# A second queue for the experts' down matrices: ACT asks for them, SP for the gate and up parts

## The reference

```python
def run(args):
    xi, e = args
    a, b = jnp.split(xi @ w_gu[e], 2, axis=-1)
    return (jax.nn.silu(a) * b) @ w_down[e]
```

## Time and profile before

| what | value |
|---|---|
| median of three runs | 842.99 us |
| the profiled execution, whole | 844.27 us |
| its span (first to last instruction) | 842.5 us |
| PE busy | 720.6 us (86%) |
| ACT busy | 152.2 us (18%) |
| q1 (SP's queue) | 230.96 MB |
| q10 (ACT's queue) | 6.54 MB |
| mean granted clock of PE | 0.982 of full speed |

### The profile page before, as it was taken

How to read it: one execution, slowest core, us unless ns; L and a number is a source line. 1 busy time by engine, 2 the same in 40 slices (tenths; PEclk the granted TensorE clock), 3 DMA queues, 4 the chain that set the end, 5 groups by cost and what they waited for, 6 DMA issues and landing times.

```text
span 842.5 us, 10234 instructions
## 1 busy us (share of the span) xinstructions
PE 720.6 (86%) x3647; PEld 373.2 (44%) x3647; DVE 203.0 (24%) x575; ACT 152.2 (18%) x363; POOL 182.4 (22%) x188
## 2 busy tenths in 40 slices
PE   6999999999988999499999997877777877877883
PEld 6788788778666446333333322222222222222220
DVE  2421305628495114710110101001001001001020
ACT  5223423033635211110000000000000000000000
POOL 5010000333000000123243241322232232232221
PEclk9999999999989999699999999999999999999998
DMA  9652942021700993499999999999999999999992
GB/s 302 123 152 69 280 159 59 1 77 34 268 1 5 391 420 140 160 348 414 408 408 417 402 406 412 418 408 414 413 408 412 416 409 412 415 414 410 415 413 73
DMA packets 76885, 246.52 MB, mean 293 GB/s; under 512 B 24944, under 2 KB 44303, under 8 KB 52235
## 3 DMA queue, kind: packets, MB, share of 16 engines
q1 hardware_dynamic: 63697, 230.96, 69.3%
q0 software_dynamic: 11776, 8.58, 4.6%
q10 hardware_dynamic: 1378, 6.54, 1.9%
HBM read 239.95 MB, written 24.92 MB: 314 GB/s over the span
## 4 chain that ended last, share of the span: by engine, by line
PE 42%; SPq 37%; DMA 9%; DVE 5%; issue 3%; ACT 2%; POOL 1%; ACTq 0%; POOLq 0%; DVEq 0%
PE bank L1111 40%; SPq L588 25%; SPq L595 11%; DMA reg_a<-in_exp_w_gu 3%; DMA reg_b<-in_exp_w_gu 3%; PE bank L1114 2%; DMA ffn_in<-reg_x 1%; DMA reg_x<-in_x_prompt 1%; DVE reg_a L1897 1%; DVE reg_y L2107 1%; DVE reg_b L1672 1%; DVE small L1857 1%; ACT reg_y L1094 0%; DVE reg_y L1904 0%; POOL small L693 0%
## 5 line engine op out<-in xcount | busy, mean ns | idle before, releaser
L1111 PE MATMUL bank<-reg_w,reg_y 128*64 128x512 f32 (+2 forms) x512 | 136.8, 572 | 15.7 <-DMA reg_w<-in_exp_w_gu 15.7
L1111 PE MATMUL bank<-reg_a,reg_y 128*64 128x512 f32 x528 | 122.8, 600 | 22.7 <-DMA reg_a<-in_exp_w_gu 17.0
L1111 PE MATMUL bank<-reg_b,reg_y 128*64 128x512 f32 x528 | 122.9, 600 | 21.4 <-DMA reg_b<-in_exp_w_gu 15.8
L2111 DVE TENSOR_TENSOR reg_y<-reg_y,bank 128x256 f32<-128x256 f32 x32 | 13.5, 421 | 417.1 <-ACT reg_y L1094 417.1
L1111 PEld LDWEIGHTS bank<-reg_w,reg_y 128*64 128x64 f32 (+2 forms) x512 | 45.3, 144 | 95.2 <-issue 54.1
L1111 PE MATMUL bank<-reg_b,reg_w 128*128 128x260 f32 x384 | 85.6, 383 | 0.0
L1111 PEld LDWEIGHTS bank<-reg_a,reg_y 128*64 128x64 f32 x528 | 34.3, 137 | 102.5 <-issue 49.4
L1111 PEld LDWEIGHTS bank<-reg_b,reg_y 128*64 128x64 f32 x528 | 34.6, 136 | 100.7 <-issue 57.8
L1111 PEld LDWEIGHTS bank<-reg_b,reg_w 128*128 128x128 f32 x384 | 72.6, 190 | 11.9 <-issue 1.0
L1114 PE MATMUL bank<-small,reg_y 128*128 128x128 f32 (+3 forms) x206 | 42.7, 317 | 24.6 <-DVE reg_y L2111 15.0
L1094 ACT ACTIVATE reg_y<-bank,small 128x256 f32<-128x256 f32 x32 | 15.2, 474 | 262.0 <-PE bank L1111 262.0
(11 more groups left out here) (357 smaller groups left out, 641.0 us busy)
## 6 DMA issues: line engine op xcount, KB each, us to landing
reg_a<-in_exp_w_gu SPq DMA_DIRECT2D x44, 1024.0 KB, 27.8
reg_b<-in_exp_w_gu SPq DMA_DIRECT2D x44, 1024.0 KB, 27.7
reg_w<-in_exp_w_gu SPq DMA_DIRECT2D x40, 1024.0 KB, 27.8
reg_a<-in_exp_w_down SPq DMA_DIRECT2D x22, 1024.0 KB, 28.1
reg_b<-in_exp_w_down SPq DMA_DIRECT2D x22, 1024.0 KB, 28.0
reg_h<-in_exp_w_down SPq DMA_DIRECT2D x20, 1024.0 KB, 27.8
reg_w<-in_w_in SPq DMA_DIRECT2D x9, 1024.0 KB, 10.7
reg_w<-in_w_out SPq DMA_DIRECT2D x2, 2048.0 KB, 11.0
```

Of the source, the lines that this page charges most:

```text
L1111: return eng.matmul(out, lhsT, rhs, start=start, stop=stop, skip_group_check=True)
L2111: tt(hid[b], silu[b], bank[2 + b][:, 256:512], ALU.mult).then_inc(S["hid_made"], 1)
```

## The change

SP no longer asks for the down matrices inside the loop. ACT gets a `load_down` of its own and asks for the two halves of expert e+3 after its silu of expert e, each behind the same wait as before, and then copies expert e's result. The loop of ACT is unrolled by six (three sets, two accumulators), with two experts ahead of it and six behind. The last three experts ask for nothing. The first three experts' matrices are still asked for by SP.

```diff
                     for g in range(3):
                         e = 3 * i + g
                         load_gu(e, g, first + e - 2)
-                        load_down(e, g, first + e - 2)
                 for e in range(N_EXP - N_EXP % 3, N_EXP):
                     load_gu(e, e % 3, first + e - 2)
-                    load_down(e, e % 3, first + e - 2)
...
-            def expert(e, n, b, reused=None):
+            def load_down(e, g, done):
+                for half in range(2):
+                    eng.wait_ge(down_half_done[half], done)
+                    src = down_dram[bass.ds(e, 1)].rearrange("e p s c n -> (e p) s c n")[:, half]
+                    eng.dma_start(down_w[g][:, half], src).then_inc(down_loaded[g][half], 16)
+
+            def expert(e, n, b, g, reused=None, more=True):
 
                 eng.wait_ge(S["gu_done"], n + 1)
                 eng.activation(silu[b], bank[2 + b][:, 0:256], ACT.Silu, scale=slot_scale[:, 1, bass.ds(e, 1)]).then_inc(S["silu_done"], 1)
+                if more:
+                    load_down(e + 3, g, n + 1)
                 eng.wait_ge(S["down_done"], n + 1)
...
-                for b in range(2):
-                    expert(b, N_EXP * r + b, b)
-                with eng.Fori(1, N_EXP // 2) as i:
-                    for b in range(2):
-                        expert(2 * i + b, N_EXP * r + 2 * i + b, b, 16 * N_EXP * r + 32 * i)
+                for e in range(2):
+                    expert(e, N_EXP * r + e, e, e)
+                with eng.Fori(0, 4) as i:
+                    for j in range(6):
+                        e = 6 * i + j + 2
+                        expert(e, N_EXP * r + e, j % 2, (j + 2) % 3, 16 * N_EXP * r + 96 * i + 32 * (j // 2) + 32)
+                for e in range(26, N_EXP):
+                    expert(e, N_EXP * r + e, e % 2, e % 3, 16 * N_EXP * r + 32 * (e // 2), e + 3 < N_EXP)
```

## The result

The changed kernel takes 851.52 us (median of four runs, 850.8 to 854.82); the kernel before took 843.65 us on the same chip. The ratio is 1.009, with an interval of 1.0066 to 1.0114: 7.9 us slower, where 7.5 were forecast. The profiled execution of the changed kernel is the longest of its four, 854.82 us with a span of 853.1. So its trace shows 10.55 us more than that of before (844.27), and its sizes are read with that in mind.

A forecast was written before the change was run, and what follows sets the result against it. The loop was taken as bound by DMA transfers without a gap. SP and ACT add 0 us and the later end 7.5 us: 842.99 + 7.5 = 850.5 us, range 840 to 862 us.

The forecast's parts named there:

- SP and ACT: Moving 58 load requests from SP to ACT in the loop was to cost or gain 0 us on either engine.
- The free price: Cost of one load request on ACT when its queue isn't held: 0.5 us, against 2.8 us when held.
- The order of the bytes: In the loop, down matrices on a second queue get half the rate, arriving in 14 us instead of 28, delaying gate and up parts.
- my sign of 12 to 16 us: Sign that the forecast is right: down halves in the loop land in 12 to 16 us instead of 28.
- The end: Gate and up parts of experts 30 and 31 come last; the last down product ends 5.5 to 8.2 us later.
- Rival A: Loop transfers: two queues feed the DMA engines better, at most 12.7 us gained, 838 us; chance 0.12.
- B: Loop loads: down halves come in the old order, so no change, 843 us; chance 0.10.
- D: Loop transfers: mixed traffic is carried worse, 381 for 412 GB/s, 24 us lost, 875 us; chance 0.08.
- C: In the loop POOL's adds become the bound, as a third queue lengthens turns: 10 us, 860 us; chance 0.12.
- the sign that I had named for C: In the loop, POOL starting its adds after a wait for the earlier ones; no size given.
- the 3 us to spare: In the loop, the time from the earlier adds' landing to POOL's start of the next expert's adds: 3 us.

## Why the prediction was right, point by point

*SP and ACT: 0 us.* Right. The kernel with 54 of 58 requests on ACT equals before. In ACT's timeline the copy follows the second request and is ready long before the next silu, as the earlier trace rows let one expect:

```profile
780.41 2.05 ACTq L1093 DMA_DIRECT2D reg_a<-in_exp_w_down  x2
782.56 0.69 ACT L1104 ACTIVATE reg_h<-bank,small 128x512 f32<-128x512 f32 x1 [5.67 <-PE bank L1120]
789.24 0.47 ACT L1098 ACTIVATE reg_y<-bank,small 128x256 f32<-128x256 f32 x1 [5.99 <-PE bank L1120]
```

The 2.05 us hold both requests, each of 0.34 us, and the wait for the down product between them. That product ended at 782.07 us, so the copy starts 0.49 us behind it, and 5.99 us stay idle before the silu. The free price was the right one to take, and a little high at 0.5 us: ACT's queue isn't held.

*The order of the bytes.* Right, in size too. I reckoned 14 us for a down matrix, 3.4 to start and 10.6 at half the rate. In the changed kernel ACT asks for one at 605.42 us; q10 moves nothing until some time in 608 to 609 us, and its last packets go in 619 to 620: some 3.4 and 10.6 us. The 11 us of the page are the median of single halves, each counted from its own request, so my sign of 12 to 16 us was set a little too high for them. Gate and up parts take 38 us. The queues of the changed kernel from 596 to 600 us (packets, MB, share):

```profile
q10 hardware_dynamic: 93, 0.76, 45.1%
q1 hardware_dynamic: 97, 0.70, 42.5%
q0 software_dynamic: 96, 0.11, 15.7%
```

Three queues take turns packet by packet, 93 to 97 to 96: each gets one turn in three, whether its packet is large or one of POOL's small ones. That each DMA engine goes round its queues packet by packet is the rule in the Trainium skill, "DMA: Bandwidth & Descriptors", section "Queues, rings and completion order", and the trace agrees.

*The end.* Right as a mechanism. One queue with the same fault at its end loses 5.8 and 9.4 us, two queues with the end in order lose nothing. Term by term, in the first profile: expert 29 complete at 806.36 us against 802.8 to 805.5; its way to the end of its down product 8.93 against 7.73 us, with the clock at 0.50; two more experts 25.77 against 25.34 us; sum 841.06 against 835.9 to 838.6. In the profile where the clock stays up on this stretch and the time is nearer to the median (852.29 us) the last down product ends at 838.53, at the upper edge of the forecast and some 11 us after the transfers, where 9 to 12 were forecast; in the other two profiles of the changed kernel it is 13 to 14 us. What follows it takes 853.1 - 841.06 = 12.0 us, before 842.5 - 830.41 = 12.1: unchanged, as said.

That the sum came out so near is partly luck, for two of its terms missed in opposite ways. I had the last down matrix asked for 8.2 us ahead of expert 29's last part, and 1.1 MiB of it missing then. In the first profile ACT asks for it from 793.22 us on, 13 us ahead, as that part comes late itself, and q10 moves only some 0.2 MB after 806 us. And I took up to one MiB off because most of the 16 engines would be ahead by then; but from 806.36 us to the transfers' end at about 828 lie 21.6 us, some 2.6 us for each of the 8.2 MiB that were left, so there was hardly anything to take off. One term too large by about a MiB and one taken off that wasn't there gave the lower edge of my 21.5 to 24.2 us, which is what came.

*Rival A* falls: 412 GB/s from 560 to 620 us, as before, and the transfers end no earlier. *B* falls: down halves land in 11 us. *D* falls: 412 GB/s with both queues at work. *C* came nearer than I gave it credit for. POOL's waits in the changed kernel (total us, times, longest):

```profile
POOL out_y_p L761 <- DMA out_y_s<-reg_y,reg_h: 97.4, 10, 10.9
...
POOL out_y_p L761 <- DMA out_y_s<-reg_h: 58.1, 6, 11.4
```

In 16 waits it was the earlier adds that POOL waited for, the sign that I had named for C; before, there was one such wait, of 8.0 us. So the turns did use up the 3 us to spare. But this sets no part of the loss: with the last two down matrices back in SP's list there are 18 such waits and no loss, and with half as many adds there is one such wait and a loss of 8.0 us.

*What stays open.* The kernel with two down matrices early lost 9.4 us where 6 us, up to some 7.6, had been expected. Its last down product ends at 840.37 us instead of 836.8. Of these 3.6 us some 1 is the later end of the transfers, and 0.6 the last expert, which takes 13.29 us from the end of the down product before (827.08 us) instead of 12.67. Its expert 30 was complete at 819.34 us; by the 2.66 us per MiB 4 MiB before its transfers' end at 828 us it would be 817.4. Why its last part let PE on 2 us later than that I didn't settle. Nor is it settled why the kernel with one down matrix early loses 5.8 us in the median and not 4.3.

## What to carry to other kernels

Where the DMA engines had no gap, as here, a second queue didn't bring the whole of the bytes sooner; it changed which of them came first, and it gave equal turns without regard to need. So ask what work follows the last byte: here 3.4 us of PE followed a down matrix, and 11 to 14 us the gate and up parts in the three profiled executions, and the difference is about the loss. If loads are to be spread over queues, let the last ones stay in one queue in the order of use.

## What the runs showed that I had not expected

The clock granted to PE fell from 1.00 to 0.50 (2.4 to 1.2 GHz) in or behind some of the longer waits for loads: in the changed kernel behind one of 2.55 us at 769 us and one of 3.20 us at 806 us, in the one-queue kernel beside one of 4.78 us at 817 us. But not behind all: a wait of 3.40 us left it at 1.00 in another execution of the changed kernel. The first of these in the changed kernel, where eight products took 3.58 us instead of 1.94:

```profile
769.17 3.58 PE L1120 MATMUL bank<-reg_a,reg_y 128*64 128x512 f32 x8 [2.55 <-DMA reg_a<-in_exp_w_gu]
```

```profile
769.00:772.00 3.00, 2.83 (x8) 0.69 (x8) 0.00 (x0) 0.00 (x0) 2.69 (x2) 0.55 1.04 430
```

Before, no wait for such a part was longer than 1.0 us, and the clock was 1.00 from 560 to 620 us. The changed kernel's mean clock is 0.947 against 0.982, which looks like the cause of the loss and isn't: one kernel here has the low clock without the loss, another the loss without the low clock.
